# Attention heads of a long and a short tile by turns, and the input transposed and modulated column block by column block under adaLN's transfers

## The reference, cut to what is computed

```
mod = silu(c) @ w_ada + b_ada                    # sh1, sc1, ga1, sh2, sc2, ga2
h = rms_norm(x, g_pre_mix) * (1 + sc1) + sh1
z = h @ w_in                                     # 2628 columns: dq dk dv | sq sk sv | iq ik iw
# 4 differential heads: (softmax(q1 k1 + bias) - lam * softmax(q2 k2 + bias)) @ v, rms_norm per head
# 8 sparse heads over 2 key heads: score = sum_h w_h relu(iq_h . ik); the best 256 visible keys of a
#   query are kept, softmax over them with bias, @ v
# a query sees the keys of its own and of earlier chunks of 64
x = x + ga1 * rms_norm(o @ w_out, g_post_mix)
h = rms_norm(x, g_pre_ffn) * (1 + sc2) + sh2
x = x + ga2 * rms_norm((silu(g) * u) @ w_down, g_post_ffn)
```

## Time and profile before

| | us |
|---|---|
| median of 3 runs | 1692.29 (1691.99 to 1693.32) |
| the profiled execution | 1689.51 |
| its span | 1687.7 |
| start of the projection's first chunk on PE | 68.5 |
| attention, first to last slot | 401 to 764 |
| output projection and feed-forward | 765 to 1687 |

### The profile page before, as it was taken

How to read it: one execution, slowest core, us unless ns; L and a number is a source line. 1 busy time by engine, 2 the same in 40 slices (tenths; PEclk the granted TensorE clock), 3 DMA queues, 4 the chain that set the end, 5 groups by cost and what they waited for, 6 DMA issues and landing times.

```text
span 1687.7 us, 24106 instructions
## 1 busy us (share of the span) xinstructions
PE 1540.6 (91%) x9123; PEld 1319.3 (78%) x9123; DVE 756.0 (45%) x1760; ACT 551.8 (33%) x1133; POOL 420.6 (25%) x366
## 2 busy tenths in 40 slices
...
GB/s 276 100 45 27 111 168 227 189 67 98 52 117 123 121 129 131 91 155 38 76 129 131 53 26 50 50 26 73 25 50 50 25 57 42 50 50 25 0 1 124
DMA packets 147336, 142.50 MB, mean 84 GB/s; under 512 B 11981, under 2 KB 129038, under 8 KB 147258
## 3 DMA queue, kind: packets, MB, share of 16 engines
...
...
## 4 chain that ended last, share of the span: by engine, by line
PE 80%; DVE 8%; issue 3%; ACT 3%; DMA 2%; POOL 2%; SPq 1%; DVEq 0%; POOLq 0%; ACTq 0%
PE S L1976 31%; PE PJ L1735 14%; PE T L1999 10%; PE PJ L1999 5%; PE S L1840 4%; DVE sc L1541 3%; PE S L1937 3%; PE PJ L1937 3%; PE T L1815 2%; PE PJ L1915 2%; DMA ada_more<-in_w_ada 1%; DVE scrap L1362 1%; PE S L1754 1%; PE S L1684 1%; ACT aT L1127 1%
## 5 line engine op out<-in xcount | busy, mean ns | idle before, releaser
L1976 PE MATMUL S<-h2h,gh 128*128 128x352 f32 (+1 forms) x1056 | 348.0, 330 | 7.4 <-POOL gl L896 4.0
L1976 PE MATMUL S<-h2h,gl 128*128 128x352 f32 (+1 forms) x1056 | 347.0, 329 | 0.0
L1976 PE MATMUL S<-h2l,gh 128*128 128x352 f32 (+1 forms) x1056 | 346.8, 328 | 0.0
L1647 DVE TENSOR_TENSOR hv<-sg,S 128x352 f32<-128x352 f32 (+1 forms) x66 | 35.0, 532 | 490.2 <-ACT sg L1271 478.1
L1976 PEld LDWEIGHTS S<-h2h,gh 128*128 128x128 f32 x1056 | 199.7, 189 | 8.4 <-issue 7.9
L1976 PEld LDWEIGHTS S<-h2l,gh 128*128 128x128 f32 x1056 | 200.5, 190 | 0.4
L1976 PEld LDWEIGHTS S<-h2h,gl 128*128 128x128 f32 x1056 | 199.5, 189 | 0.0
L1362 DVE TENSOR_SCALAR_CACHE_REDUCE scrap<-work,cand 128x384 uint8<-128x384 f32 (+6 forms) x217 | 180.1, 884 | 1.1
L1735 PE MATMUL PJ<-hTh,wh 128*128 128x352 f32 (+3 forms) x504 | 168.0, 333 | 0.0
L1999 PE MATMUL T<-dh,ahl 128*128 128x512 f32 x504 | 166.6, 390 | 0.0
L1735 PE MATMUL PJ<-hTl,wh 128*128 128x352 f32 (+3 forms) x504 | 165.4, 328 | 0.0
...
## 6 DMA issues: line engine op xcount, KB each, us to landing
...
```

What stands on the lines that cost most here:

```text
L1976: last = pe.matmul(S[u % 2][:, 512 * part:512 * part + n], wp[slot][:, k, 128 * part:128 * part + 128], hp[:, k, c0:c0 + n], start=(k == 0 ...
```

## The change

Two parts. **In the head** all nine tiles of x stay in SBUF (xin has nine buffers) and are loaded first, then the two weight blocks, then the eight ada blocks, each into its own place, in pairs (0,4), (1,5), (2,6), (3,7): shift and scale of the same 256 columns of the model. The transposes of x run before adaLN; xT holds x in columns of tokens for each of the eight blocks k of the width. After a pair of ada blocks DVE modulates the two k that it serves (modulated), ACT makes their high part (high_x), DVE their low part, and PE adds these two k to five chunks at once, (0,0), (0,1), (0,2), (1,0), (1,1), in five PSUM banks (FIRST_CHUNKS, first_chunks), one pair late. The transposes of the cached keys move from before block 0's last chunk to block 2.

**In attention** the order of slots is a table: tiles 4, 5, 6, 7 in odd places of the list, tiles 0, 1, 2, 3 in the even ones, tile 8 last. With d for the four differential steps and s for the four sparse ones, the eight groups of eight slots are 4d/0d, 5d/0s, 4s/1d, 5s/1s, 6d/2d, 6s/2s, 7d/3d, 7s/3s, each by turns. Ties are settled in the order 4, 5, 6, 2, 7, 3, 8 at slots of a table; the 40 search parts are laid over 33 points in place of 39, since tile 4 needs them by slot 11. The values of all eight tiles are loaded at once, the queries go into four buffers.

```diff
-LATE_POINTS = 3 * 13
+LATE_POINTS = 3 * 11
-    return j % 4 if j < ADA_FIRST else j % 2
+ADA_PAIRS = [(j, ADA_FIRST // 2 + j) for j in range(ADA_FIRST // 2)]
+FIRST_CHUNKS = [(0, 0), (0, 1), (0, 2), (1, 0), (1, 1)]
-EARLY = {5: 0, 8: 1}
+LONG = [(t, i) for t, half in ((4, 0), (5, 0), (4, 1), (5, 1), (6, 0), (6, 1), (7, 0), (7, 1))
+        for i in range(4 * half, 4 * half + 4)]
+SHORT = [(t, i) for t in range(4) for i in range(8)]
+ORDER = [step for pair in zip(LONG, SHORT) for step in pair] + [(8, i) for i in range(8)]
+TIE_ORDER = [4, 5, 6, 2, 7, 3, 8]
+TIE_SLOT = {4: 11, 5: 18, 6: 32, 2: 36, 7: 48, 3: 52, 8: 64}
...
+            def modulated(i):
+                k = 2 * i
+                dve.wait_ge(ada_cols, 2 * i + 2)
...
+                for kk in (k, k + 1):
+                    for g, rows in enumerate((slice(0, SEQ), slice(SEQ, TOK))):
+                        last = nc.vector.tensor_scalar(xT[:, kk, rows], xT[:, kk, rows], scaleA[:, 0, kk, g:g + 1],
+                                                       modT[:, kk, g:g + 1], ALU.mult, ALU.add)
+                    last.then_inc(x_modulated, 1)
+                for kk in (k, k + 1):
+                    dve.wait_ge(x_hi, kk + 1)
+                    nc.vector.tensor_tensor(hTl[:, kk, :], xT[:, kk, :], hTh[:, kk, :].bitcast(F32), ALU.subtract
+                                            ).then_inc(x_lo, 1)
...
+            for t in range(NT):
+                transpose_x(t)
...
+            for i, pair in enumerate(ADA_PAIRS):
+                for part, j in enumerate(pair):
+                    ada_products(j, 2 * i + part)
+                    ada_transposes(j, 2 * i + part)
                 if i:
+                    first_chunks(i - 1)
+            first_chunks(len(ADA_PAIRS) - 1)
```

More of the change, by code:

```diff
@@ L154, in tie_stage @@
 def tie_stage(slot, lag):
-    t, rest = divmod(slot + 2 - lag, 8)
-    return t if t in TOPK_TILES and rest == 0 else None
+    return next((t for t in TIE_ORDER if TIE_SLOT[t] + lag == slot), None)
 def late_parts(slot, point):
@@ L291, in build @@
         prow = place("prow", [97, 128], F32, base[0] - 512)
-        vt = place("vt", [128, 2, KB, 128], F32, base[0] - 2 * NT * 128 * 4)
-        xin = place("xin", [128, 2, D], F32, late)
-        xn = then("xn", [128, 2, D])
         work_off = 45312
@@ L467, in build @@
         pchain = sem("pchain")
[L468 to L469 removed]
+        x_hi = sem("x_hi")
+        x_lo = sem("x_lo")
         w_hi = sem("w_hi")
@@ L627, in _ @@
             load_x(1)
-            for j in range(4):
-                load_ada(j)
+            sp.dma_start(tab[:, :], I["tab"]).then_inc(ld_tab, 16)
+            sp.dma_start(onehot[:, :], I["onehot"]).then_inc(ld_tab, 16)
+            for t in range(2, NT):
+                load_x(t)
+            load_w(0)
+            load_w(1)
+            for pair in ADA_PAIRS:
+                for j in pair:
+                    load_ada(j)
             for i, name in enumerate(("lq1", "lk1", "lq2", "lk2")):
@@ L1306, in _ @@
+            for i in range(len(ADA_PAIRS)):
+                modulated(i)
             dve.wait_ge(ld_lam, 64)
@@ new lines, in chunk_rows, with first_chunks @@
+            def chunk_rows(b, c, k):
+                c0, n = CHUNKS[c]
+                w = BLOCKS[b][3]
+                for p, (wp, hp) in enumerate(((wh, hTh), (wh, hTl), (wl, hTh))):
+                    last = pe.matmul(chunk_bank(3 * b + c)[0:w, 0:n], wp[:, b % 2, k, 0:w], hp[:, k, c0:c0 + n],
+                                     start=(k == 0 and p == 0), stop=(k == KB - 1 and p == 2))
+                if k == KB - 1:
+                    last.then_inc(chunk_done, 1)
+            def first_chunks(i):
+                if i == 0:
+                    pe.wait_ge(r_out, 3)
+                for k in (2 * i, 2 * i + 1):
+                    pe.wait_ge(x_lo, k + 1)
+                    for b, c in FIRST_CHUNKS:
+                        if k == 0 and c == 0:
+                            pe.wait_ge(w_lo, b + 1)
+                        chunk_rows(b, c, k)
```

463 lines of the change are left out of this document (234 added, 229 removed).

## The result

| | before | after |
|---|---|---|
| median of 16 runs, us | 1691.07 (1689.22 to 1693.39) | 1694.55 (1688.82 to 1699.07, and one run of 2626.84) |
| profiled execution / its span | 1689.51 / 1687.7 | 1695.16 / 1693.3 |
| sixth chunk (1,2) starts | 98.77 | 77.77 |
| first bias of attention | 401.04 | 385.46 |
| attention, first bias to output projection | 363.3 | 385.1 |

The changed kernel takes 1.0016 times the time of before, 95% interval 1.001 to 1.0023: slower by 0.16%, an amount that the noise does not hide but that is small. The run of 2626.84 us had a granted clock of 0.645 over the whole program, and it is left out of this ratio. The forecast was 1677, the range ended at 1691. The head gained what was forecast, and attention gave it all back.

The account below looks back on a forecast made before the run. PE bounds projection and feed-forward; head and attention were open, with DVE's order chaining attention's slots. Head -17 and attention +2 turn the profiled 1689.5 into 1674.5; the median, 2.8 above that execution, gives 1677 us, range 1663 to 1691.

Parts of the forecast that it names:

- I take 80: Head: the first five chunks end at 80 us, between 77.1 and 85.6, a gain of 17 us.
- rival 4: Head: each portion of chunk matmuls starts at the low clock, end 85.6, time 1683 us; chance 0.12.
- Rival 3: Head: all its chunks run at 1.2 GHz, so it gains 0 to 3 us, time 1691; chance 0.10.
- 2 us longer, give or take 13: Attention as a whole: the new slot order makes it 2 us longer, uncertain by 13 us.
- with 4.7 and 5.8 us of ties in the two differential groups: Attention, groups 6d/2d and 7d/3d: totals of 40.4 and 45.7 us said to include 4.7 and 5.8 of ties.
- 12.4 a pair, 65 us for eleven slots: Attention, slots 0 to 10: a 4d/0d pair with search parts takes 12.4 us, the eleven slots 65.
- rival 2: Attention: the clock stays at 1.2 GHz, adding 19 us (1696) and 21 more if low to slot 31; chance 0.13.
- it decides from slot 16: Attention: a clock still low at slot 16 makes 4s/1d pairs take 11.6 us in place of 6.7.
- PEclk 0.5 beyond slot 16: Attention: the sign named for the clock staying low, a granted PE clock of 0.5 after slot 16.
- 7.7, 9.5, 10.7 a pair: Attention, sparse groups 5s/1s, 6s/2s and 7s/3s: set by PE, at 7.7, 9.5 and 10.7 us a pair.
- covered: Attention's start: value loads delay the fifth bias load some 8 us, but it is needed only 22 us after the first slot.
- Rival 1: Attention: turns hide waits, winning a third of PE's 0.7 us idle a slot, -15 us, time 1662; chance 0.15.

Follow-up runs that it names:

- e5_values_spread: New head with attention tile by tile, values loaded one tile ahead instead of all at once, later queries at slot 8; 1674.26 us, ratio 0.9906.
- e13_ties_earlier: Changed kernel with the ties of tiles 6, 2, 7, 3 and 8 at earlier slots; 1687.20 us, ratio 0.9971.
- e1: Changed kernel with its new head and loads, but attention's slots tile by tile as before; 1678.05 us, ratio 0.9919.
- e9: Changed kernel with four of the search's five late rounds left out; 1682.74 us in one execution.
- e10: e5_values_spread, tile by tile, with four of the search's five late rounds left out; 1660.45 us in one execution.
- e12: e9 with eight added PE products in slots whose own step is differential and that turn a differential output; 1688.17 us in one execution.
- e14: Changed kernel with groups 4d/0d, 6d/2d and 7d/3d run one after the other, other groups still by turns; 1687.02 us, ratio 0.9972.
- e11: Changed kernel once more, unchanged, for a second trace; 1690.18 us in one execution.
- e6: Changed kernel with five added PE products only in slots whose own step is differential and that turn a differential output; 1690.51 us, ratio 0.9994.

## Why the prediction was wrong

**Right: the head.** "I take 80" for the sixth chunk; it began at 77.8, and at 74.3 to 80.5 in the fourteen other traces with this head. Here only the first portion started slow; in some executions a second or third one did too, which is a part of rival 4, though with an end at 79 us and not at 85.6. Rival 3 did not come. With e5_values_spread the whole head is worth 1691.35 - 1674.26 = 17.1 us, as forecast (17). That it fits to 0.1 us is luck, since single terms were off and cancelled: the three table products took 2.1 us, not 4.2; pair 0 ended at 37.7 (39.5); pair 1 at 48.0 (48.1), where DVE's modulation took 3.60 us, twice what I had (its first piece took 2.44 us, while POOL worked on the low weights and then on small memsets, and 0.81 in the next pair without them); the transposes went on in 1.06 us for eight from 23 us on, though the first eight took 1.97. The sentence on the Trainium skill (TensorE: Matmul & The Clock Gate, Part 4: PE-mode transpose) gave them the slow pace throughout; the trace disagrees. One reading was off too: chunk (0,1) of before began at 79.55, so its short spans at 83.76 came after 4.2 us of chunk work and not 3.

**Wrong: attention, "2 us longer, give or take 13"; it is 21.8 longer.** By groups, forecast and measured: slots 0 to 10 65 and 67.1; 11 to 15 23.5 and 26.1; 16 to 31 61 and 67.3; 6d/2d 40.4 and 45.7; 6s/2s 38 and 40.4; 7d/3d 45.7 and 49.6; 7s/3s 43 and 44.2; tile 8 47.4 and 44.8. Every group by turns is above its sum. Slots 0 to 63 are 23.7 us above the forecast of 316.6, and tile 8 is 2.6 below.

The step that failed in the second half is the term "with 4.7 and 5.8 us of ties in the two differential groups". Four pairs of 9.6 and 10.7 us are 38.4 and 42.8, so the 40.4 and 45.7 hold only 2.0 and 2.9 us for these ties; more than half of them was put at nothing, and no reason was given. The trace has 5.9 and 6.6 us of them on the chain. I also had all of slots 32 to 63 at 2.4 GHz, since the earlier trace rows show 1.00 for these tiles. But before, compares stood in sparse steps, where DVE waits for PE anyway. Between a short and a long differential slot the compare delays the one thing PE needs next, PE pauses 1.8 us, the clock falls, and the long scores come 1.3 us later: e13_ties_earlier shows 6.1 us for one compare of 2.84, the shift of the other ties by a slot, and the dips that went with them. The two groups are 9.2 us of the 23.7 above their forecast, and the ties on the chain are 7.6 above what the sum held for them. My chain of the pair itself, 10.7 us, was not too short: with the clock at 1.00 group 7d/3d takes 43.5 in e13, under my 45.7.

The sums of the first half failed by 10.9 us (149.5 forecast, 160.4 measured), and there only parts have a cause. "12.4 a pair, 65 us for eleven slots" is wrong as a sum: five and a half such pairs are 68, and 67.1 were measured.

**Half right: rival 2.** It was the slow side, and the clock has a part in it, but at the wrong place: "it decides from slot 16", and slots 16 to 31 are at 1.00. The clock was low up to slot 9 as expected, rose to 0.83 in slots 12 to 15, and fell again in slots 32 to 39 and 48 to 55, which I had not considered since nothing was slow there before. "PEclk 0.5 beyond slot 16" was too coarse a sign to look for.

**Wrong, and smaller.** The sparse groups by turns (7.7, 9.5, 10.7 a pair) take 8.7, 10.4 and 11.8 from one long slot to the next, once they run evenly. I had summed PE's work alone; PE waits once a pair for ACT's copy (0.94) and once for DVE's second scaling of the long tile (0.42), which stands behind the short tile's bias. The value loads, "covered", are covered only as long as the first five slots last 22 us: in e1 they cost 4.3. Rival 1 had a real part, 12 us less waiting for POOL, but the idle of 0.7 us a slot that it wanted to use was not won; that steps at distance two are of one tile is the likely reason, argued from the code.

**Open.** The first half costs 8.2 us more than tiles 0, 1, 4 and 5 before, and with the search cut short the loss is all in slots 0 to 15. It isn't the search (e9, e10) and added work on PE doesn't give it back (e12). That long tiles now run their scores and transposes at 1.2 GHz there would fit, but no run shows it. In the second half the loss is 14.7 us; slots 32 to 63 take 170.5 us in e13 and 168.7 in e14, after 179.9 (176.8 in e11), so each takes most of it away, in traces that are among the fastest of their kernels. The compare's place and the alternation act together; their shares, and the clock's beside them, can't be told apart.

**The spread.** The changed kernel's runs lie between 1688.8 and 1699.1, those of before within 4.2 us. The sixth chunk's start moved by 6 us between executions of one and the same head, and the number of dips in 6d/2d changes the group between 42.6 and 45.7. A single profiled execution of such a kernel is good to some 5 us.

## What to carry to other kernels

Price a moved step by who waits behind it in its new place, not by its own length: in e13 2.8 us more of DVE in the sparse group 6s/2s cost 1.0 us, and about the same between two differential slots that PE waits for had cost 6. Before steps are laid by turns, follow the software pipeline: what runs at distance two is then always of the same kind, and nothing long meets anything short. And a full clock is a fact of the order that a stage had, not of the stage: here it fell in two groups in which it had been full, behind a pause of PE of 1.8 us in one place and of at most 1.06 us in two others, while in e13 a pause of 1.05 us left it full.

## What the runs showed of the chip beyond that

- More work made a kernel a little faster: with 5 products of 0.14 us added in the differential slots (e6) the ratio went from 1.0016 to 0.9994, and groups 6d/2d and 7d/3d took 90.1 us, against 95.4 and 92.2 without.
- What the clock level is worth differs by stage: 0.51 to 0.77 in tiles 0 and 1, with ten products added a slot, moved 0.3 us of 70.9.
- In the head, DVE's modulation of four pieces of xT took 3.60 us beside POOL's low weights (38.35 to 39.68) and memsets (to 40.3), and 1.98 us for the next pair, with POOL idle. In eight other traces of this head the same pieces took 3.44 or 3.60 us and then 1.98 or 1.99:

```profile
38.43 3.60 DVE L1394 TENSOR_SCALAR xT<-xT,scaleA,modT 128x1024 f32<-128x1024 f32 x4
...
48.68 1.98 DVE L1394 TENSOR_SCALAR xT<-xT,scaleA,modT 128x1024 f32<-128x1024 f32 x4
```

- Eight transposes of x, early and late in a stretch that holds only such transposes on PE:

```profile
10.46 1.97 PE L1770 MATMUL T<-ident,xin 128*128 128x128 f32 x8 [5.39 <-DVE xin L1358]
...
23.14 1.06 PE L1770 MATMUL T<-ident,xin 128*128 128x128 f32 x8 [0.70 <-DVE xT L1365]
```
